# Small attention operands padded to 128 by 128 in a two-block transformer kernel

## Time and profile before

| | |
|---|---|
| Median of three runs | 2324.66 us |
| Profiled execution, its own time | 2329.18 us |
| Span of the profile, first to last instruction | 2327.5 us |
| PE busy | 2302.8 us, 99% |
| PEld (weight loads) busy | 2011.7 us, 86% |
| DVE busy | 1926.3 us, 83% |
| ACT busy | 1185.9 us, 51% |
| Mean DMA rate | 221 GB/s |
| Mean granted PE clock | 0.997 |

### The profile page before, as it was taken

One profiled execution on the slowest core, in us unless ns is written; L12 is line 12 of the kernel. 1 busy time (PEld: TensorE's weight loads), 2 busy tenths in 40 slices (PEclk: granted clock), 3 DMA queues, 4 the chain that ended last, 5 costly groups with the idle time before them and its releaser, 6 DMA issues.

```text
span 2327.5 us, 36572 instructions
## 1 busy us (share of the span) xinstructions
PE 2302.8 (99%) x13706; PEld 2011.7 (86%) x13706; DVE 1926.3 (83%) x3112; ACT 1185.9 (51%) x1719; POOL 109.5 (5%) x208
## 2 busy tenths in 40 slices
PE   8999999999999999999999999999999999999998
PEld 7888788888888888888898888889988888888887
DVE  7987768899999999999989867898777677777777
ACT  6544555565445454544456657556634434434444
POOL 0000000000111111111010000000000000000000
PEclk9999999999999999999999999999999999999999
DMA  8556653468888888888885563554555555555552
GB/s 308 181 194 233 213 201 139 170 243 293 287 299 293 293 299 286 307 285 303 284 281 186 206 232 110 172 192 181 182 194 183 182 192 187 182 189 190 181 186 104
DMA packets 86268, 513.64 MB, mean 221 GB/s; under 512 B 9669, under 2 KB 10229, under 8 KB 37216
## 3 DMA queue, kind: packets, MB, share of 16 engines
q1 hardware_dynamic: 57312, 406.88, 48.8%
q0 software_dynamic: 28656, 104.33, 13.4%
q10 hardware_dynamic: 144, 0.26, 0.0%
HBM read 509.30 MB, written 2.13 MB: 220 GB/s over the span
## 4 chain that ended last, share of the span: by engine, by line
PE 95%; DVE 2%; ACT 1%; DMA 1%; issue 0%; DVEq 0%; SPq 0%; ACTq 0%
PE ps L564 49%; PE ps L565 25%; PE ps L562 5%; PE ps L561 2%; PE ps L557 2%; PE ps L558 2%; PE ps L559 2%; PE ps L617 2%; PE ps L627 1%; PE ps L646 1%; PE ps L698 1%; PE ps L636 1%; DVE wl L1533 1%; DMA modraw<-in_wmod 1%; ACT wh L973 0%; PE ps L584 0%
## 5 line engine op out<-in xcount | busy, mean ns | idle before, releaser
L973 ACT ACTIVATE wh<-raw 128x1024 fp32r<-128x1024 f32 x766 | 809.2, 1058 | 718.4 <-PE ps L562 486.2
L1533 DVE TENSOR_TENSOR wl<-raw,wh 128x1024 fp32r<-128x1024 f32 x762 | 929.9, 1222 | 193.5 <-ACT wh L973 177.7
L564 PE MATMUL ps<-xs,wh 128*128 128x512 f32 x2720 | 973.8, 399 | 0.4 <-DVE tk_a L1568 0.4
L565 PE MATMUL ps<-xs,wl 128*128 128x256 f32 x2720 | 762.6, 280 | 0.0
L564 PEld LDWEIGHTS ps<-xs,wh 128*128 128x128 f32 x2720 | 511.0, 188 | 118.4 <-issue 5.4
L565 PEld LDWEIGHTS ps<-xs,wl 128*128 128x128 f32 x2720 | 513.6, 189 | 9.9
L1606 DVE CUSTOM_DVE_ANT_0 modraw<-modraw,cb 128x1024 f32<-128x1024 f32 x192 | 233.2, 1219 | 15.4 <-DMA modraw<-in_wmod 15.1
L564 PE MATMUL ps<-xc,wh 128*128 128x512 f32 x616 | 222.0, 399 | 0.0
L1593 DVE SCALAR_TENSOR_TENSOR x<-ps,mod,x 128x256 f32<-128x256 f32 x320 | 154.7, 484 | 65.1 <-PE ps L562 58.8
L564 PE MATMUL ps<-hs,wh 128*128 128x512 f32 x560 | 200.9, 398 | 0.0
L565 PE MATMUL ps<-xc,wl 128*128 128x256 f32 x616 | 173.3, 281 | 0.0
(11 more groups left out here) (339 smaller groups left out, 3207.0 us busy)
## 6 DMA issues: line engine op xcount, KB each, us to landing
raw<-in_w SPq DMA_DIRECT2D x381, 1024.0 KB, 5.0
modraw<-in_wmod POOLq DMA_DIRECT2D x192, 512.0 KB, 4.7
x<-in_x SPq DMA_DIRECT2D x4, 512.0 KB, 8.7
raw<-in_w SPq DMA_DIRECT2D x4, 512.0 KB, 8.8
tbias<-rel_rows POOLq DMA_DIRECT2D x4, 512.0 KB, 10.1
out_dram<-y SPq DMA_DIRECT2D x4, 512.0 KB, 2.9
cb<-c_silu POOLq DMA_DIRECT2D x1, 1024.0 KB, 4.8
hmask<-in_hmask SPq DMA_DIRECT2D x1, 512.0 KB, 17.0
```

What stands on the lines that cost most here:

```text
L564: nc.tensor.matmul(out[:, :], hi[:, w], pair, start=s, stop=e)
L565: m = nc.tensor.matmul(out[:, 0:T], lo[:, w], xh, start=False, stop=e, skip_group_check=e)
L973: nc.scalar.activation(wh[:, h % HS, :], raw[:, u % RAW, (h % 2) * 1024:(h % 2 + 1) * 1024], ACT.Copy).then_inc(s_round, 1)
L1533: nc.vector.tensor_tensor(wl[:, h % HS, :], raw[:, (h // 2) % RAW, (h % 2) * 1024:(h % 2 + 1) * 1024], wh[:, h % HS, :].bitcast(F32), ALU. ...
```

## The change

Every small operand listed above gets 128 rows and 128 columns, with zeros in the rows that carry nothing, except the gate-sum transposes.

- SWA keys stand twice, in two tiles of 128 rows: head group 0 in the upper 64 rows with zeros below, group 1 the other way round. The query tile of two heads is used whole. Values are used as whole blocks of both groups (128 columns), and the step reads only its 64 output rows.
- The shared rope key of MLA is made into two half tiles in the same way.
- The key term of fox is stacked: -F rounded in rows 0 to 5, the rest in rows 32 to 37 of a zeroed fp32r tile `fkey`, times a column of `pick`. It becomes one record instead of two.
- The hgrn spread does the same (`apair`), at step `H_END + 4` instead of `H_END + 3`. One strip and one `pick` serve hgrn and both head norms; they are made at step `H_PICK` = 42.

```diff
-        into = lambda j, n: strip[:, 2 * B_H - 1 - j:2 * B_H - 1 - j + n]
-        into2 = lambda j: strip2[:, 2 * B_H - 1 - j:2 * B_H - 1 - j + HROWS]
-        spread2 = lambda j: pick[:, j:j + 1].to_broadcast([HROWS, P])
-        spread = lambda j, n: ident[0:n, j:j + 1].to_broadcast([n, P])
+        into = lambda j: strip[:, 2 * B_H - 1 - j:2 * B_H - 1 - j + P]
+        spread = lambda j: pick[:, j:j + 1].to_broadcast([P, P])
+        low_rows = lambda n: slice(32, 32 + n)
...
-                                          (sel.to_broadcast([B_H, P]), fnp[:, 1, 0:keys(t)])],
+                                          (spread(h), fkey[:, 0:keys(t)])],
...
-            return dict(scores=lambda t: [(sec2[r, SWA_Q[h // 2], qt(t)], sec2[r, SWA_K, 0:keys(t)])],
+            return dict(scores=lambda t: [(sec2[:, SWA_Q[h // 2], qt(t)], sec2[:, SWA_K[h % 2], 0:keys(t)])],
...
-                        v=[vt[:, 0, q * P + kv * SWA_D:q * P + (kv + 1) * SWA_D] for q in range(2)],
-                        rows=r, out=mix[r, h // 2, :])
+                        v=[vt[:, 0, qt(q)] for q in range(2)], rows=r, out=mix[r, h // 2, :])
...
-                                          (lat[r, QR + h // 2, qt(t)], sec2[r, KR, 0:keys(t)])],
+                                          (lat[:, QR + h // 2, qt(t)], sec2[:, KR_HALF[h % 2], 0:keys(t)])],
...
-                            mm = nc.tensor.matmul(PS[6][0:HROWS, 0:T], into2(2 * j + q), hsq[:, j % 2, q * T:(q + 1) * T],
+                            mm = nc.tensor.matmul(PS[6][:, 0:T], into(2 * j + q), hsq[:, j % 2, q * T:(q + 1) * T],
...
-                            m = nc.tensor.matmul(PS[7][d["rows"], qt(t)], d["v"][q], probT[:, J % 2, qt(t + q)],
+                            m = nc.tensor.matmul(PS[7][:, qt(t)], d["v"][q], probT[:, J % 2, qt(t + q)],
...
-                if i == H_END + 3:
+                if i == H_END + 4:
                     pe.wait_ge(s_hv, HV["rstd"])
                     for h in range(A_H):
-                        m = nc.tensor.matmul(PS[4 + h // 2][:, (h % 2) * T:(h % 2 + 1) * T], spread(h, A_H),
-                                             kk[0:A_H, 0, :], start=True, stop=True)
+                        m = nc.tensor.matmul(PS[4 + h // 2][:, (h % 2) * T:(h % 2 + 1) * T], spread(h),
+                                             apair[:, :], start=True, stop=True)
...
+            def in2_bias(j):
+                if j != SWA_K[0]:
+                    add_bias("in2", j, sec2[:, j, :])
+                    return
+                act.wait_ge(s_scl, SCALED["in2"] + j + 1)
+                for r, k in zip(KEY_ROWS, SWA_K):
+                    m = nc.scalar.activation(sec2[r, k, :], tb[r, j % 2, 0:T], ACT.Identity, bias=tb[r, j % 2, T:T + 1])
+                m.then_inc(s_evac, 1)
...
+                if i == H_PICK:
+                    dve.wait_ge(s_const, 48)
+                    link(nc.vector.memset(strip[:, :], 0.0),
+                         nc.vector.tensor_scalar(pick[:, :], causal[:, 0:2 * B_H], 0.0, None, ALU.mult),
+                         nc.vector.tensor_scalar(fkey[:, :], causal[:, :], 0.0, None, ALU.mult))
+                    for o in (0, 32):
+                        rows = slice(o, o + 2 * B_H)
+                        nc.vector.tensor_copy(pick[rows, :], ident[rows, rows])
+                        nc.vector.memset(strip[:, 2 * B_H - 1 + o:2 * B_H + o], 1.0).then_inc(s_pick, 1)
...
-                    nc.vector.reciprocal(kk[0:A_H, 0, :], kk[0:A_H, 0, :]).then_inc(s_hv, 1)
+                    link(nc.vector.reciprocal(kk[:, 0, :], kk[:, 0, :]))
+                    link(nc.vector.tensor_copy(apair[:, :], kk[:, 0, :]))
+                    low = low_rows(A_H)
+                    nc.vector.tensor_tensor(apair[low, :], kk[low, 0, :], apair[low, :].bitcast(F32), ALU.subtract
+                                            ).then_inc(s_hv, 1)
...
-                    nc.vector.tensor_scalar(fnp[:, 1, :], fnp[:, 0, :], -1.0, None, ALU.mult).then_inc(s_qk, 1)
+                    hi = fkey[0:B_H, :]
+                    link(nc.vector.tensor_scalar(hi, fsum[:, :], -1.0, None, ALU.mult))
+                    nc.vector.scalar_tensor_tensor(fkey[low_rows(B_H), :], fsum[:, :], -1.0, hi.bitcast(F32),
+                                                   ALU.mult, ALU.subtract).then_inc(s_qk, 1)
...
+                    link(nc.vector.memset(sec2[KEY_ROWS[1], SWA_K[0], :], 0.0),
+                         nc.vector.memset(sec2[KEY_ROWS[0], SWA_K[1], :], 0.0))
...
-                    nc.vector.tensor_tensor(b, rtmp[:, 0, :], rtmp[:, 1, :], ALU.add).then_inc(s_kvr, 1)
+                    if r:
+                        nc.vector.tensor_tensor(b, rtmp[:, 0, :], rtmp[:, 1, :], ALU.add).then_inc(s_kvr, 1)
+                    else:
+                        for rows, k in zip(KEY_ROWS, KR_HALF):
+                            nc.vector.tensor_tensor(sec2[rows, k, :], rtmp[rows, 0, :], rtmp[rows, 1, :], ALU.add)
+                        nc.vector.memset(sec2[KEY_ROWS[1], KR, :], 0.0).then_inc(s_kvr, 1)
```

More of the change, by code:

```diff
@@ L115 @@
 H_V, H_LV, H_STEP, H_GATE = 28, 28, 4, 38
+H_PICK = H_GATE + 4
 H_END = H_LV + H_STEP * (len(LVL) + 1)
@@ L207, in build @@
         gtmp = at("gtmp", [B_H, T], T0 + 17)
-        fnp = at("fnp", [B_H, 2, T], T0 + 18)
+        fsum = at("fsum", [B_H, T], T0 + 17)
+        fkey = at("fkey", [P, T], T0 + 18, F32R)
         hsq = at("hsq", [P, 2, 512], T0)
[L211 to L214, removed]
+        hrs = at("hrs", [P, T], T0 + 4)
+        hpair = at("hpair", [P, T], T0 + 5, F32R)
+        strip = at("strip", [P, 2 * B_H - 1 + P], T0 + 19)
+        apair = at("apair", [P, T], T0 + 1, F32R)
+        pick = at("pick", [P, 2 * B_H], T0 + 19.625, F32R)
         hsq4 = at("hsq4", [P, 4, T], 136)
@@ L593, in head_norm @@
                         for q in range(2):
-                            mm = nc.tensor.matmul(PS[4 + j % 2][:, q * T:(q + 1) * T], spread2(2 * j + q),
+                            mm = nc.tensor.matmul(PS[4 + j % 2][:, q * T:(q + 1) * T], spread(2 * j + q),
                                                   hpair[:, :], start=True, stop=True)
@@ L670, in hgrn @@
                     pe.wait_ge(s_ha, HA["sq"])
+                    pe.wait_ge(s_pick, 2)
                     for h in range(A_H):
-                        m = nc.tensor.matmul(PS[4][0:A_H, 0:T], into(h, A_H), kq[:, h, :], start=h == 0, stop=h == A_H - 1)
+                        m = nc.tensor.matmul(PS[4][:, 0:T], into(h), kq[:, h, :], start=h == 0, stop=h == A_H - 1)
                     m.then_inc(s_hp, 1)
-                if i == H_END + 3:
+                if i == H_END + 4:
                     pe.wait_ge(s_hv, HV["rstd"])
                     for h in range(A_H):
-                        m = nc.tensor.matmul(PS[4 + h // 2][:, (h % 2) * T:(h % 2 + 1) * T], spread(h, A_H),
-                                             kk[0:A_H, 0, :], start=True, stop=True)
+                        m = nc.tensor.matmul(PS[4 + h // 2][:, (h % 2) * T:(h % 2 + 1) * T], spread(h),
+                                             apair[:, :], start=True, stop=True)
                     m.then_inc(s_hp, 1)
@@ L735, in fox @@
                         for t in range(2):
-                            m = nc.tensor.transpose(PS[7][:, B_H * t:B_H * (t + 1)], fnp[:, 0, qt(t)], ident[0:B_H, 0:B_H])
+                            m = nc.tensor.transpose(PS[7][:, B_H * t:B_H * (t + 1)], fsum[:, qt(t)], ident[0:B_H, 0:B_H])
                         m.then_inc(s_fT, 1)
@@ L1082, in head_norm @@
                     act.wait_ge(s_hss, 6 * m + 6)
-                    nc.scalar.activation(hrs[:, :], PS[6][0:HROWS, 0:T], ACT.Sqrt, scale=1.0 / HD,
-                                         bias=col("eps")[0:HROWS, :]).then_inc(s_hrms, 1)
+                    nc.scalar.activation(hrs[:, :], PS[6][:, 0:T], ACT.Sqrt, scale=1.0 / HD, bias=col("eps")).then_inc(s_hrms, 1)
             def v_copy(n, g, bank=None):
@@ L1183, in hgrn @@
                     act.wait_ge(s_hp, HP["var"])
-                    nc.scalar.activation(kk[0:A_H, 0, :], PS[4][0:A_H, 0:T], ACT.Sqrt, scale=1.0 / HD,
-                                         bias=col("eps")[0:A_H, :]).then_inc(s_ha, 1)
+                    nc.scalar.activation(kk[:, 0, :], PS[4][:, 0:T], ACT.Sqrt, scale=1.0 / HD, bias=col("eps")).then_inc(s_ha, 1)
             for i in range(2 * FIRST_BLOCKS):
@@ L1708, in head_norm @@
                     link(nc.vector.tensor_copy(hpair[:, :], hrs[:, :]))
-                    low = slice(32, HROWS)
+                    low = low_rows(2 * B_H)
                     nc.vector.tensor_tensor(hpair[low, :], hrs[low, :], hpair[low, :].bitcast(F32), ALU.subtract
@@ L1755, in _ @@
             nc.vector.memset(ones[:, :], 1.0).then_inc(s_ones, 1)
-            link(nc.vector.memset(strip, 0.0))
-            nc.vector.memset(into(0, 1), 1.0).then_inc(s_ones, 1)
-            dve.wait_ge(s_ones, 2)
             dve.wait_ge(s_par, 16)
```

33 lines of the change are left out of this document (10 added, 23 removed).

## The result

The changed kernel took 2304.77 us (median of six runs, 2303.93 to 2306.14), the kernel before 2325.93 beside it (six runs, 2324.50 to 2327.88). The ratio is 0.991, 95% interval 0.9897 to 0.9922: 0.9% faster, 21.2 us by the medians. The profiled executions took 2304.02 and 2329.18, 25.2 us apart. A repeat further down gives 0.9904 (0.9888 to 0.9921), 23.5 us by the medians. Forecast were 24.7 us and 2300.0.

The account below looks back on a forecast made before the run. PE's own instruction sequence was taken as the bound. Step gains of 28.2 us less 0.5, 0.5 and 2.5 given back made 24.7 net: profiled execution 2304.5, median 2300.0 us, range 2295.0 to 2307.0.

Parts of the forecast that it names:

- The bound: Whole kernel: PE's own sequence sets the end, so time taken out of it comes off the end.
- The price of a form: PE's small steps: each change of operand form costs 0.09 on entry and about 0.10 behind, whatever the operand's size.
- 64 or fewer: PE's small products: the extra cost appears wherever the rows or columns used fall to 64 or fewer.
- rival 3: Widened operands: their longer weight loads show, 152 records by at most 0.10, 15.2 us off the gain, 2315.2; chance 0.01.
- Sums, hgrn spread, fox, MLA: Head square sums, hgrn spread, fox scores and MLA rope steps: PE gains of 2.1, 1.9, 7.1 and 6.3 us.
- the selectors: Made at half 42 of hgrn, no longer before the first head sums: gain 0.4 us, bounds 0 and 0.8.
- The 128-column rounded record without a row: Fox key term: cost of one 128-column fp32r record, between half of 0.12 and 0.12, taken at 0.12.
- Spreads of the head norms: L594, six groups of four: gain 2.25 us, less 0.5 lost in the first norm to DVE's scaling.
- SWA with the latents: SWA scores and values beside the latent projections: gain 8.1 us, of which 2.5 turns into waits for ACT and DVE.
- Rival 1: SWA and latents become bound by DVE and ACT, all 8.1 lost and 1 more: gain 18.1, 2306.6 us; chance 0.13.
- Added DVE work: Extra DVE operations and one ACT bias, some 4 us if uncovered: 0.5 counted, for zeroings and rope key.
- The level: Profiled execution from 2329.2 to 2304.5 us, median from 2324.7 to 2300.0, 1.1% less.

Follow-up runs that it names:

- the widths run: Changed kernel with head sums at 96 columns, head spreads at 96 rows, hgrn sum at 64 columns and hgrn spread at 64 rows: 2307.87 us.
- The three banks: Changed kernel with the head spreads going round three PSUM banks instead of two: 2303.67 us (one run).
- the last experiment: DVE's scaling of query block 11 put ahead of its half's job step, against the changed kernel with three spread banks and later modulation slices: 2298.55 us, ratio 0.9886.
- the stop of 5.0: Changed kernel with two modulation slices loaded ahead of the four bias transfers of the second block's input stage: 2308.75 us (one run).

## Why the prediction was right, and where its sizes were off

**The bound.** PE's sequence set the end: of the 26.8 us by which its busy time fell, 25.1 came off the span.

**The price of a form.** Right in size for the steps it was read from, and in kind. It hangs on the change and not on the records (1.92 against 2.32 with the same four small records), and it falls in two parts, 0.10 on entry (0.33 for 0.23) and the rest behind. The 0.19 to 0.20 for both parts hold for rows; for columns a change costs 0.14 to 0.17. What the prediction put at "64 or fewer" is bounded by the widths run: free at 96, full at 64. The wider weights cost nothing in any step at full shape, so rival 3 falls.

**Sums, hgrn spread, fox, MLA.** 0.34 + 1.19 + 0.93 = 2.46 with the selectors against 2.1 + 0.4; then 1.88, 7.08 and 6.35 against 1.9, 7.1 and 6.3. The 128-column rounded record without a row, bounded by 0.06 and 0.12 and taken at 0.12, costs about 0.12: two key records add 297.04 - 296.16 - 0.65 = 0.23 to a fox step.

**Spreads of the head norms: the mis-sized term.** 2.25 less 0.5 was forecast, 0.30 came. The prediction saw that L594 already waited for DVE's scaling in the first norm and let "between 0 and 0.75" be lost. It lost 0.93 of 1.125 there, and in the second norm, for which nothing was taken off, 1.0 of 1.125. Before, PE's middle spreads started 1.28 and 1.27 behind the start of DVE's scaling in the two norms; after, PE came to them 0.78 and 0.43 behind it, and the scaling of two blocks lasts 1.40. PE had come forward against DVE by 0.5 and 0.8, and DVE held the bank. The three banks gave 1.26 back and so confirm the place for that part. The step that failed is the reading of one short wait in one norm as the only tight place: the other norm is the same code with a slack that the waits of before do not list. So the term for what the head norms give back was mis-sized: 0.5 forecast, 1.95 measured.

**SWA with the latents.** 2.5 was taken off, and 8.1 - 5.17 = 2.9 went; in three half units 2.6: 1.67 where the stop is, 0.49 and 0.43 where the scores wait for the next and the previous block of queries (0.44 and 0.16 listed). The size was near, the place was not: it was forecast that L627 would grow from 0.6 to some 3, but it stayed at 0.6, and the scores got a wait of 1.3. Rival 1, DVE and ACT as the bound of the whole stage with all 8.1 lost, is refuted by the 5.17 gained, and by the last experiment, which kept all their work, changed only its order and gained 1.46 more.

**Added DVE work.** 0.5 was taken, nothing shows. The two zeroings of half keys stand ahead of an idle DVE; its timeline after:

```profile
1329.20 0.27 DVE L2153 MEMSET sec<- 64x256 f32 x1
1329.59 0.27 DVE L2154 MEMSET sec<- 64x256 f32 x1
1335.81 1.23 DVE L1609 CUSTOM_DVE_ANT_0 modraw<-modraw,cb 128x1024 f32<-128x1024 f32 x1 [5.95 <-DMA modraw<-in_wmod]
```

**The level.** The sum made the profiled execution 2304.5, and it took 2304.0. That it came so close is luck: the spreads lost 1.5 us more than forecast and SWA 0.4 more, and the 2.14 at the entry, which was not forecast, and the DVE work that was hidden made up for them. The change itself gave 23.0 of the 24.7. The median came out at 2304.8 and not 2300.0, since the 4.5 us by which the profiled run before lay above its median was taken over unchanged. That run had the stretch at half clock; after, the profiled run had none and lies 0.75 below its median. The kernel before took 2324.6, 2325.9, 2326.5 and 2328.6 as a median in four series of six or seven runs, so the gain by medians is uncertain by some 2 us, and 2300.0 was taken from the low end.

## What to carry to other kernels

A small product that stands alone between full-size ones pays for its form twice, on entry and on the way back, and not for its size: pad it with zeros where the zeros cost nothing, or put small ones next to each other. Before counting a gain on the busiest engine as a gain in time, measure how late each other engine's result comes at the steps around it, also where no wait is listed: a lead of zero and a long lead look the same in the waits. And when such a wait then appears, look for one operation behind another in an in-order engine before calling that engine the bound.

## What the runs showed of the hardware

- A small product between full ones costs a pair of changes, in and out: 0.38 to 0.39 us for 64 rows (MLA, SWA, the hgrn spread), 0.27 to 0.34 for 64 or fewer columns (SWA values, the sums), about 0.10 of it before the first record. 96 rows and 96 columns cost what 128 do.
- Narrow value products saved nothing: with 64 columns an SWA step took 0.27 more than with whole blocks of 128.
- A stop of PE of 1.3 to 2.2 us was followed in some profiles by 3.4 us at a granted clock of 0.50, worth 1.5 to 1.6 where the stop was as long as in the changed kernel, and in others, with the same stop at the same place, by none. As an estimate from this, two such places spread a kernel's time by some 3 us. Behind the stop of 5.0 PE ran at half clock for 6.8 us.
